# Three column blocks of x turned by 32x32 blocks ahead of a layer's end, in a pooling and retention trunk on one core

## What is computed

```python
D_MODEL = 2048; BATCH = 1; SEQ = 256; DEPTH = 2; D_FF = 4 * D_MODEL
def rmsnorm(x, g):
    y = x * lax.rsqrt(jnp.mean(x * x, axis=-1, keepdims=True) + EPS)
    return y * g
def modulate(h, shift, scale):
    return h * (1 + scale[:, None, :]) + shift[:, None, :]
def reference(x, c, ...):
    for i in range(DEPTH):
        h = modulate(rmsnorm(x, norm_g[i, 0]), shift_t, scale_t)
        y = pool_mixer(h, ...) if i % 2 == 0 else retention(h, ret_w_in, ret_w_out)
        x = x + gate_t[:, None, :] * y
        h = modulate(rmsnorm(x, norm_g[i, 1]), shift_m, scale_m)
        x = x + gate_m[:, None, :] * sq_relu_mlp(h, mlp_w1[i], mlp_w2[i])
    return rmsnorm(x, final_g)
```

## Time and profile before

| | before |
|---|---|
| median of 3 runs | 2337.22 us (2337.05 to 2338.13) |
| span of the profiled execution | 2336.1 us (its own time isn't listed apart from the three) |
| PE busy | 2251.9 us, 96% of the span |
| DVE busy | 1681.1 us, 72% |
| ACT busy | 1084.2 us, 46% |
| POOL busy | 139.9 us, 6% |
| mean granted TensorE clock | 0.987 of full speed |
| first end: last matmul of the MLP to first matmul of retention | 893.38 to 896.57 us |
| second end: the same between retention and the second MLP | 1625.04 to 1628.22 us |

### The profile page before, as it was taken

How to read it: one execution, slowest core, us unless ns; L and a number is a source line. 1 busy time by engine, 2 the same in 40 slices (tenths; PEclk the granted TensorE clock), 3 DMA queues, 4 the chain that set the end, 5 groups by cost and what they waited for, 6 DMA issues and landing times.

```text
span 2336.1 us, 28515 instructions
## 1 busy us (share of the span) xinstructions
PE 2251.9 (96%) x10033; PEld 1817.7 (78%) x10033; DVE 1681.1 (72%) x1814; ACT 1084.2 (46%) x1342; POOL 139.9 (6%) x249
## 2 busy tenths in 40 slices
PE   4489999999999999999999999999999999999998
PEld 2147788888888887888888888887888888888887
DVE  4668889788887898777676767677877555555557
ACT  2324554544544545444454444555553453453454
POOL 0000000100100100001000001000100000000000
PEclk9689999999999999999999999999999999999999
DMA  9999989998998977888766887876997776776774
GB/s 400 415 413 393 339 297 328 364 367 277 368 334 292 362 281 231 303 264 275 246 233 215 299 260 244 273 239 202 333 359 248 235 230 195 226 232 191 232 228 152
DMA packets 276674, 664.21 MB, mean 284 GB/s; under 512 B 21768, under 2 KB 22200, under 8 KB 269632
## 3 DMA queue, kind: packets, MB, share of 16 engines
q1 hardware_dynamic: 260320, 611.92, 75.8%
q0 software_dynamic: 15328, 49.87, 6.2%
q10 hardware_dynamic: 896, 0.75, 0.1%
HBM read 638.30 MB, written 24.14 MB: 284 GB/s over the span
## 4 chain that ended last, share of the span: by engine, by line
PE 88%; DMA 2%; DVE 2%; ACT 1%; issue 0%; POOLq 0%; POOL 0%; SPq 0%; DVEq 0%; ACTq 0%
PE acc L701 86%; DMA raw<-in_mlp_w 2%; PE acc L1122 1%; DVE w_lo L1601 1%; PE score_ps L1109 0%; ACT w_hi L1173 0%; DVE ada_acc L1607 0%; PE score_ps L908 0%; PE tb L848 0%; DVE ev L1903 0%; PE tb L983 0%; DVE x L1907 0%; DVE scratch L1773 0%; DVE scratch L1768 0%; PE mod_ps L856 0%
## 5 line engine op out<-in xcount | busy, mean ns | idle before, releaser
L1601 DVE TENSOR_TENSOR w_lo<-raw,w_hi 128x1024 fp32r<-128x1024 f32 x775 | 943.3, 1223 | 558.6 <-ACT w_hi L1173 555.5
L1173 ACT ACTIVATE w_hi<-raw 128x1024 fp32r<-128x1024 f32 x775 | 821.8, 1061 | 1094.8 <-PE acc L701 971.5
L701 PE MATMUL acc<-w_hi,h_lo 128*128 128x512 f32 x1788 | 698.5, 391 | 2.6 <-issue 1.6
L701 PE MATMUL acc<-w_hi,h_hi 128*128 128x512 f32 x1788 | 695.8, 389 | 0.0
L701 PE MATMUL acc<-w_lo,h_hi 128*128 128x512 f32 x1788 | 695.8, 389 | 0.0
L701 PE MATMUL acc<-w_hi,a_lo 128*128 128x512 f32 x1308 | 511.6, 391 | 0.4 <-DVE w_lo L1601 0.4
L701 PE MATMUL acc<-w_lo,a_hi 128*128 128x512 f32 x1308 | 510.3, 390 | 0.0
L701 PE MATMUL acc<-w_hi,a_hi 128*128 128x512 f32 x1308 | 510.0, 390 | 0.0
L701 PEld LDWEIGHTS acc<-w_hi,h_lo 128*128 128x128 f32 x1788 | 335.7, 188 | 75.1 <-issue 4.1
L701 PEld LDWEIGHTS acc<-w_hi,h_hi 128*128 128x128 f32 x1788 | 335.7, 188 | 70.0
L701 PEld LDWEIGHTS acc<-w_lo,h_hi 128*128 128x128 f32 x1788 | 335.8, 188 | 68.5
(11 more groups left out here) (216 smaller groups left out, 912.9 us busy)
## 6 DMA issues: line engine op xcount, KB each, us to landing
raw<-in_mlp_w SPq DMA_DIRECT2D x512, 512.0 KB, 5.1
ada_raw<-in_ada_w SPq DMA_DIRECT2D x248, 512.0 KB, 6.6
raw<-in_ret_w_in SPq DMA_DIRECT2D x192, 512.0 KB, 4.6
ada_early_h<-in_ada_w SPq DMA_DIRECT2D x32, 1024.0 KB, 13.4
raw<-in_ret_w_out SPq DMA_DIRECT2D x64, 512.0 KB, 4.4
ada_raw<-in_ada_w SPq DMA_DIRECT2D x16, 1024.0 KB, 12.5
square_blocks<-ev POOLq DMA_DIRECT2D x112, 128.0 KB, 4.8
ev<-square_blocks POOLq DMA_DIRECT2D x28, 512.0 KB, 6.4
```

The source lines that it names most:

```text
L701: mm = nc.tensor.matmul(acc[pair][t][:], l[:, CK * c + j, tok], w[:, slot, j, :], start=first and j == 0 and i == 0, stop=last and j == CK ...
L1173: nc.scalar.activation(w_hi[:, o % RING], raw[:, o % RING], ACT.Copy).then_inc(hi_ready, 1)
L1601: nc.vector.tensor_tensor(w_lo[:, o % RING], raw[:, o % RING], w_hi[:, o % RING].bitcast(F32), ALU.subtract).then_inc(lo_ready, 1)
```

## The change

Column blocks 0, 1 and 2 of x are complete before the end is reached; only block 3 is not. The change takes these three blocks, unscaled, through the way by memory ahead of the end: ACT copies a block in block order into a buffer of `scratch` (`copy_block`), DVE turns it (`turn_block`), POOL sorts it through DRAM (`turn_x`). At the end they have only to be multiplied by the inverse roots. As the tokens now lie along the free axis, the roots are needed as a row in all partitions: DVE puts them on a diagonal (`diagonal`), PE multiplies ones by it into PSUM (`spread_root`), and DVE multiplies the sorted block by that row (`scale_turned`). ACT then reads its fill from `scratch` and not from PSUM. Block 3 goes the old way (fills 5 and 7). `TURNED_FILLS` is 3.

```diff
+        x_blocks = [scratch[:, 2048:3072], scratch[:, 4096:5120], scratch[:, 1024:2048]]
...
             def first_unit(kind, pair, lhs, free):
-                fills_after = ({1: (2,), 2: (3, 4), 3: (5,)}, {1: (6,), 3: (7,)})
-                fill(0)
-                fill(1)
+                after = ({1: [lambda: spread_root(1)], 3: [lambda: fill(5)]}, {3: [lambda: fill(7)]})
+                spread_root(0)
...
+            def spread_root(t):
+                if t == 0:
+                    pe.wait_ge(tevac, n.of("TB"))
+                    pe.wait_ge(tlo, n.of("TL"))
+                pe.wait_ge(diag_ready, 1 + n.n["XS"] // 4 + t + 1)
+                nc.tensor.matmul(root_rows[t], ones[:], diag[:, t, :], start=True, stop=True).then_inc(root_row, 1)
...
+            def copy_block(b):
+                for t in range(TT):
+                    nc.scalar.activation(x_block_order(b, t),
+                                         x[:, t, b * NB:(b + 1) * NB].rearrange("p (k r j) -> p r k j", k=4, r=4),
+                                         ACT.Copy).then_inc(xb_copied, 1)
...
                                 if u == 6:
                                     hooks[1] = [lambda: block_squares(0, 1)]
-                                    hooks[4] = [lambda: block_squares(1, 0)]
+                                    hooks[4] = [lambda: block_squares(1, 0), lambda: block_copied(0)]
+                                    hooks[5] = [lambda: block_copied(1)]
                                 else:
+                                    hooks[0] = [lambda: block_copied(2)]
                                     hooks[2] = [lambda: block_squares(2, 0)]
...
+            def turn_block(b):
+                dve.wait_ge(xb_copied, (n.n["XS"] // 8 * TURNED_FILLS + b + 1) * TT)
+                nc.vector.transpose(x_blocks[b], x_blocks[b]).then_inc(xb_turned, 1)
+
+            def scale_turned(q):
+                t, f = FILLS[q]
+                dve.wait_ge(root_row, n.n["XS"] // 4 + t + 1)
+                dve.wait_ge(xb_in, 16 * (n.n["XS"] // 8 * TURNED_FILLS + f + 1))
+                row = root_rows[t].rearrange("p (o q i) -> p o q i", o=1, q=4).to_broadcast([P, 4, 4, 32])
+                nc.vector.tensor_tensor(x_sorted(f, t), x_sorted(f, t), row, ALU.mult).then_inc(xs_ready, 1)
...
+                            if first == 3 and layer == 0 and u == 6:
+                                hooks.setdefault(5, []).append(lambda: turn_block(0))
+                                hooks.setdefault(7, []).append(lambda: turn_block(1))
                             if last:
+                                if layer == 0:
+                                    hooks.setdefault(0, []).append(lambda: turn_block(2))
                                 hooks.setdefault(3, []).append(other_groups_added)
...
+                        if r == 1 and i > 12:
+                            hooks.setdefault(0 if last else 4, []).append(lambda i=i: turn_block(i - 13))
...
+            def turn_x(i):
+                there, block_ = x_sorting[i % 2], x_blocks[i % TURNED_FILLS]
+                pool.wait_ge(xb_turned, i + 1)
+                for q in range(4):
+                    pool.dma_start(there[:, :, q, :].rearrange("r j n -> j r n"),
+                                   block_[32 * q:32 * q + 32].rearrange("p (r n) -> p r n", r=4)).then_inc(xb_out, 16)
+                pool.wait_ge(xb_out, 4 * 16 * (i + 1))
+                if i:
+                    pool.wait_ge(xb_in, 16 * i)
+                pool.dma_start(block_, there.rearrange("r j q n -> (r j) (q n)")).then_inc(xb_in, 16)
...
             turn_group(2)
+            turn_x(0)
             spread_gate(gate[:], 1)
+            turn_x(1)
+            turn_x(2)
             tile_roots()
...
+            for i in range(TURNED_FILLS, 2 * TURNED_FILLS):
+                turn_x(i)
             tile_roots()
```

More of the change, by code:

```diff
@@ L472, in by_blocks, with x_block_order, x_sorted @@
             return half[:, 4 * w:4 * w + 4, t * P:(t + 1) * P].rearrange("p k (q i) -> p k q i", q=4)
+        def x_block_order(b, t):
+            return x_blocks[b].rearrange("p (r t k j) -> p t r k j", r=4, t=TT, k=4)[:, t]
+        def x_sorted(b, t):
+            return x_blocks[b].rearrange("p (q t k i) -> p t k q i", q=4, t=TT, k=4)[:, t]
+        root_rows = [tb[t][:, 0:P] for t in range(TT)]
         gate_bias_rows = seg_row[0:32, 0:64]
@@ L811, in first_unit @@
                         chunk(c, *lhs, pair, c == 0, False, (t,))
-                        for q in fills_after[t].get(c, ()):
-                            fill(q)
+                        for step in after[t].get(c, ()):
+                            step()
                 n.add(XS=2 * 4, HT=2 * CH)
                 unit(kind, pair, {}, lhs, ready_h, free, HALF, CH)
+            def spread_root(t):
[4 more added lines that the diff above has]
+                nc.tensor.matmul(root_rows[t], ones[:], diag[:, t, :], start=True, stop=True).then_inc(root_row, 1)
             def fill(q):
@@ L1502, in block_squares, with block_copied @@
                                 squares(i - 13)
+                            def block_copied(i=i):
+                                act.wait_ge(x_added, n.of("XA") * TT)
+                                copy_block(i - 13)
                             hooks[2] = [block_squares]
+                            if r == 1:
+                                hooks.setdefault(0 if last else 3, []).append(block_copied)
                         steps(hooks, 0 if last else LEAD - (i == R_UNITS - 1))
@@ L1873, in boundary @@
                 lo(1)
-                scale_x(0)
+                diagonal(0)
                 gated(1)
-                scale_x(1)
+                scale_turned(0)
                 added(1)
+                scale_turned(1)
                 split_part(0, 0)
@@ L1882, in boundary @@
                 split_part(1, 0)
-                scale_x(2)
-                scale_x(3)
-                scale_x(4)
+                diagonal(1)
+                split_part(1, 1)
+                scale_turned(2)
                 lo(3)
-                split_part(1, 1)
+                scale_turned(3)
                 split_part(2, 0)
+                scale_turned(4)
+                split_part(2, 1)
                 scale_x(5)
-                split_part(2, 1)
-                scale_x(6)
+                scale_turned(6)
                 split_fill(3)
```

29 lines of the change are left out of this document (23 added, 6 removed).

## The result

The change makes the kernel slower: 2358.16 us in the median of five runs (2356.29 to 2358.44) against 2337.22 (2336.50 to 2338.13) for five of the kernel before on the same chip. The ratio is 1.0087, with a 95% interval of 1.0076 to 1.0098, so about 20.9 us. The forecast was 2349.7 with a range to 2357.5: the direction was right, the size was 8.5 us short, and the range missed the time by 0.7.

What follows compares the result with a forecast made beforehand. PE was taken as the bound, with DVE busy in the ends' holes and POOL holding the first root. First end 10.4 - 0.7 + 1.4 = 11.1 us, second 1.4: 12.5 more, 2349.7 us on the median, range 2341.5 to 2357.5.

Steps and rivals of the forecast that it cites:

- POOL's queueing: First end, POOL's one DMA queue: transfers wait for those ahead; 4 us taken, upper bound 6.4, putting the root at 902.7.
- the half clock: PE after its 12 us hole at the first end: four us at half clock cost its stream 2, absorbed, so nothing added.
- DVE's own term: Bridge from root to chunk 4, each end: DVE's dearer multiplications and two diagonals, 1.6 us more work, chunk 4 1.4 later.
- "-0.7": First end: DVE's low part, which held the scaling 0.7 us behind the root, is long done, so 0.7 us is subtracted.
- What bounds the kernel: Whole kernel: PE has 88% of the chain of waits, so time counts only where PE stops or its work changes.
- POOL holds the first root: First end: POOL's serial sort, gate row, sort, sort delays the first root by 10.4 us, to 902.7.
- A second delay behind POOL's: MLP's last unit: ACT's third copy waits for block 2's addition, root 1.8 us late; costs nothing while POOL is late.
- POOL in time: First end: root starts within 3 us of 892; +4.6 us in all, 2341.8 us; chance 0.14.
- PE as the bound of the bridge: Both ends: PE's fills are the bridge's price, so the kernel is faster by 1 to 4.7 us, around 2334.5; chance 0.05.
- Starved weights: The change's DMAs, 1 MB more per block, delay weights: 6 to 8 us over the forecast, 2357; chance 0.06.
- The third block: Behind the root: PE waits for the third sorted block, whose read lands too late; 2353 us; chance 0.03.

Runs made afterwards that it cites:

- the kernels with and without the transposes: 18 unread PE transposes in the hole: added to the change at the second end alone, 2342.40 to 2338.98 us; to both ends, root ahead of third sort's wait, 2344.39 to 2342.13.
- the one with the gate row behind: The change with the gate row and its 1 MB load issued behind the first end's roots, not between first and second sort: 2348.28 us, ratio 1.0038.
- the kernel with the copy later: Both ends turned, root ahead of third sort's wait, idle transposes; block 2's copy and turn moved behind the last unit's third chunk: 2341.55 us, ratio 1.0016.
- the four kernels with the root moved up: The change, gate row behind roots, first root ahead of third sort's wait: 2344.39 us; plus idle transposes 2342.13; those plus later copy 2341.55; instead, low part earlier 2344.27.
- the root moved up and the clock kept: The change with gate row behind the roots, first root ahead of the third sort's wait, 18 idle transposes at both ends: 2342.13 us, ratio 1.0019.
- the half-size multiplications: The change at the second end alone with idle transposes, each of six row multiplications covering two of four column groups: 2337.51 us, ratio 0.9999.
- the first-end kernel: The change at the first end only (MLP to retention), the second end as in the kernel before: 2356.00 us, ratio 1.0075.

## Why the prediction was right in sign and short in size

Two steps of the sum failed. POOL's queueing was put at 4 us and measured 7.4, and the half clock was put at nothing and delayed DVE, the bound, at both ends by 1.1 us. What is left of the shortfall is DVE's own term, 1.4 against 1.8 to 2.0, and the "-0.7".

- **What bounds the kernel**: right. The page's shares hardly moved, and 20.0 us lie in the two ends, against 20.9 between the medians.
- **POOL holds the first root, in the order sort, gate row, sort, sort**: right in mechanism, short in size. The step that failed is the queueing, "I take 4" of a "bound from above" of 6.4. Without queueing I had 26.1 us from the first sort's issue to the root; measured are 904.97 - 871.46 = 33.5, so 7.4 us stand where the term of 4 stood: 3.4 more than forecast, and the bound was not one. Of the 7.4, the 4.9 of the second sort are shown to come from the gate row and its load ahead of it; whether by their place in the queue or by their share of the DMA engines, no run tells. The first sort took 7.0 (7.6 forecast), the gate row 4.3 from issue to its wait's end (3.0), the second sort's writes 11.4 (6.6 and queueing), the third's 8.6 (6.6). "Since the DMA engines are nearly idle there, 0.14 busy" is where it went wrong: that is one stretch, 890 to 894, put in for a queue of 30 us. The stretches ahead of it in the trace of before were there to be read, and 884 to 888 is full of retention's first weights:

```profile
884.00:888.00 4.00, 4.00 (x20) 3.30 (x19) 3.88 (x8) 0.05 (x1) 0.00 (x0) 1.00 1.03 386
888.00:892.00 4.00, 4.00 (x19) 3.33 (x18) 2.57 (x4) 2.21 (x4) 0.00 (x0) 1.00 0.22 84
```

In the change the same weights and POOL's transfers share the engines up to 900:

```profile
888.00:892.00 4.00, 4.00 (x19) 3.29 (x19) 3.75 (x9) 1.67 (x3) 0.00 (x0) 1.00 0.93 357
...
896.00:900.00 4.00, 0.00 (x0) 0.00 (x0) 0.79 (x1) 2.11 (x2) 1.99 (x4) 0.60 0.88 258
```

- **The half clock, "I add nothing"**: wrong. I had seen the clock fall behind the first hole, but set it only against PE's own stream, which had room. What it delays is the second root's row: PE makes it behind two chunks, and DVE, the bound, waits 1.85 us for it at the first end and 1.39 at the second, where I had foreseen no lowered clock at all. It costs 1.1 to 1.3 us a bridge by the kernels with and without the transposes, and 0.6 and 2.2 in the one with the gate row behind.
- **"-0.7" for the low part that no longer holds the scaling**: half of it shows at first and none at chunk 4. The first chunk starts 4.50 us behind the late root, and 4.85 behind the second end's, where no such gain was forecast (4.25 and 4.26 before). The diagonal follows the root at once (905.58 against a root's end of 905.54), but the two row matmuls behind it take 0.76 us at half clock and not 0.46, and the row behind chunk 1 is late anyway. The first bridge grew by 3.1 us and the second by 3.0.
- **DVE's term, 1.4 an end**: right mechanism, 1.8 to 2.0 at full clock. A multiplication takes 0.68 to 0.69 us, as taken from the adds of the earlier trace rows, and fill 5 makes PE wait 1.26 us where I had some 2. The line of all twelve: min, median, max, in ns.

```profile
L1910 DVE TENSOR_TENSOR scratch<-scratch,tb x12: 680/682/689, 906.8 to 1653.8; 128x512 f32<-128x512 f32 x12
```

- **A second delay behind POOL's**: right, it exists and costs nothing while POOL is late. By the kernel with the copy later it is 0.9 us on the root, forecast 1.8. ACT did stand there: the copy waited 5.40 us for the addition.

```profile
880.02 1.16 ACT L1234 ACTIVATE scratch<-x 128x512 f32<-128x512 f32 x2 [5.40 <-DVE x L1824]
```

- **Rivals.** POOL in time, 2341.8 us, did not happen, but could be made: the root moved up and the clock kept gives 2342.1. PE as the bound of the bridge is excluded by the half-size multiplications. Starved weights exist, but not with the 6 to 8 us of the rival. The MLP's last matmul comes 22.4 us from the reference point against 21.3; with the copy later it is 21.55, so most of that is the copy. Retention's first weights do come late: ACT waits 3.13 us for them, where before it waited for none of them ahead of the first chunk. Behind the late root that is covered. With the root in time 0.1 to 0.6 us is lost there: at the first end the first chunk starts 4.95 to 5.39 us behind the root in the four kernels with the root moved up, at the second 4.84 in all of them. The third block was in time.

```profile
894.48 1.06 ACT L1195 ACTIVATE w_hi<-raw 128x1024 fp32r<-128x1024 f32 x1 [3.13 <-DMA raw<-in_ret_w_in]
```

In numbers, forecast and measured: root 10.4 and 13.9, first bridge 0.7 and 3.1, second bridge 1.4 and 3.0; 12.5 and 20.0.

What stays open: how much of the sorts' time is due to the weight loads beside them. The third sort's writes took as long without the gate row ahead of them (8.9 us against 8.6), so the gate is not the cause of its length, but no kernel was run with the weights held back.

## What to carry to other kernels

When work moves to an engine that waits in program order, count what its queue already carries there, put a short instruction that others wait for ahead of each wait that it doesn't need, and put big loads that nobody needs yet behind it. Taking work from the busiest engine gains nothing in a stretch where it waits for another: here PE lost six fills an end, DVE got 0.2 us more for each, and the end became longer. Where a hole grows, ask what the engine behind it makes *for the others* at half clock, not only whether its own stream has room.

## What the runs showed of the hardware

- Holes of about three us lowered TensorE's granted clock in some profiled executions and not in others. At the unchanged ends, whose hole holds two fills, it fell in one of the six that were profiled: 1.00 before and 0.87 and 0.70 in the first-end kernel, 18.4 and 19.5 us for the same bridge. At the turned ends, whose hole holds only the row and was longer in three of them (up to 16.2 us), it fell in all ten, for a bridge of 20.65 to 22.43 us. With 2.13 us of idle transposes in the hole it stayed at 1.00 in all six turned ends that had them, for 18.79 us with the multiplications halved and 20.22 to 20.58 with them whole. At the lower level (1.2 GHz) matmuls of 512 columns were 0.43 us apart, and 0.23 at the full one.
- A load of 1 MB that spreads a row over the partitions took 9.5 us to land (7.8 before). Four writes of 128 KB issued behind it in POOL's queue took 11.4 us from the first issue to the end of the wait, where the same four took 6.5 without it. The Trainium skill, "DMA: Bandwidth & Descriptors", section on the anatomy of one DMA, would give about 4.4 us for 1 MB, as an estimate; the runs here are far above it, with the weight loads on the same engines.
